# Sample tokens' C times old state: C stationary in four column strips, the turned states moving

## The reference, cut to what matters

```python
# b = sequence, l = token, g = group (8), r = head of the group (4), p = 64, n = state (128)
y_off = jnp.einsum('bclgn,bcgrpn->bclgrp', cc.astype(jnp.float32), h_prev) * jnp.exp(a_cs)[..., None]
y = (y_diag + y_off).reshape((bsz, nc * cl) + x.shape[2:])[:, :seqlen]
# and the state that goes out
h * d_c[..., None, None] + s_c
```

## Time and profile before

| | |
|---|---|
| median of 3 runs | 2480.31 us (2479.99 to 2480.95) |
| profiled execution, span | 2479.5 us |
| PE busy in it | 2237.7 us, 90% |
| DVE, ACT, POOL busy | 52%, 40%, 17% |
| mean granted clock of PE | 0.92 |
| the SSD loops | 568 to 853 us, 1783 to 2068 us |

### The profile page before, as it was taken

How to read it: one execution, slowest core, us unless ns; L and a number is a source line. 1 busy time by engine, 2 the same in 40 slices (tenths; PEclk the granted TensorE clock), 3 DMA queues, 4 the chain that set the end, 5 groups by cost and what they waited for, 6 DMA issues and landing times.

```text
span 2479.5 us, 38482 instructions
## 1 busy us (share of the span) xinstructions
PE 2237.7 (90%) x15036; PEld 2079.1 (84%) x15036; DVE 1291.6 (52%) x1936; ACT 985.0 (40%) x1121; POOL 417.0 (17%) x162
## 2 busy tenths in 40 slices
PE   7999899988898888899989989999798889869996
PEld 5999889976677788799889989898677778869996
DVE  3553546665656472454355453576665663544543
ACT  3552434253333432454255434343432334325532
POOL 2000002211222355200000000121122223640000
PEclk9999989789888889999999999897988889989998
DMA  7444543413433333344444437442233332434441
GB/s 200 160 165 139 177 149 123 132 52 103 123 92 105 96 103 126 124 158 152 155 129 159 160 120 206 137 132 84 84 99 98 105 115 71 150 107 141 162 157 65
DMA packets 258231, 317.05 MB, mean 128 GB/s; under 512 B 9070, under 2 KB 232846, under 8 KB 258010
## 3 DMA queue, kind: packets, MB, share of 16 engines
q1 hardware_dynamic: 249656, 287.92, 36.4%
q0 software_dynamic: 7776, 26.73, 3.6%
q10 hardware_dynamic: 680, 0.80, 0.1%
HBM read 291.44 MB, written 26.33 MB: 128 GB/s over the span
## 4 chain that ended last, share of the span: by engine, by line
PE 72%; DVE 11%; PEld 5%; ACT 4%; issue 3%; POOL 3%; DVEq 1%; DMA 1%; SPq 0%; PEldq 0%; ACTq 0%; POOLq 0%
PE ps L1415 18%; PE ps L1417 17%; PE ps L1416 17%; PE ps L1516 4%; POOL w_lo L1336 3%; PE ps L1836 2%; PE ps L1832 2%; ACT w_hi L672 2%; DVE a_tri L1207 2%; DVE w_lo L923 1%; PE ps L1779 1%; PEld ps L1415 1%; PEld ps L1691 1%; PE ps L1500 1%; PEld ps L1417 1%
## 5 line engine op out<-in xcount | busy, mean ns | idle before, releaser
L1415 PE MATMUL ps<-u_hi,w_hi 128*128 128x288 f32 x2736 | 866.5, 317 | 50.0 <-DVE u_lo L950 39.7
L1416 PE MATMUL ps<-u_lo,w_hi 128*128 128x288 f32 x2736 | 848.3, 310 | 0.0
L1417 PE MATMUL ps<-u_hi,w_lo 128*128 128x288 f32 x2736 | 845.1, 309 | 0.0
L672 ACT ACTIVATE w_hi<-w_raw 128x2048 fp32r<-128x2048 f32 x249 | 476.2, 1912 | 660.7 <-PE ps L1417 634.8
L923 DVE TENSOR_TENSOR w_lo<-w_raw,w_hi 128x2048 fp32r<-128x2048 f32 x172 | 394.3, 2292 | 547.2 <-ACT w_hi L672 547.1
L1415 PEld LDWEIGHTS ps<-u_hi,w_hi 128*128 128x128 f32 x2736 | 554.7, 203 | 57.3 <-issue 53.7
L1416 PEld LDWEIGHTS ps<-u_lo,w_hi 128*128 128x128 f32 x2736 | 555.8, 203 | 0.5
L1417 PEld LDWEIGHTS ps<-u_hi,w_lo 128*128 128x128 f32 x2736 | 554.8, 203 | 0.0
L1336 POOL TENSOR_TENSOR w_lo<-w_raw,w_hi 128x2048 fp32r<-128x2048 f32 x77 | 358.0, 4649 | 626.0 <-ACT w_hi L672 625.8
L1415 PE MATMUL ps<-h_hi,w_hi 128*128 (+1 forms) x704 | 209.2, 297 | 14.6 <-DVE w_lo L923 14.6
L1417 PE MATMUL ps<-h_hi,w_lo 128*128 (+1 forms) x704 | 207.9, 295 | 0.0
(11 more groups left out here) (270 smaller groups left out, 2803.6 us busy)
## 6 DMA issues: line engine op xcount, KB each, us to landing
w_raw<-in_ffn_w_dram SPq DMA_DIRECT2D x128, 1024.0 KB, 5.0
w_raw<-in_w_in_dram SPq DMA_DIRECT2D x82, 1024.0 KB, 5.3
h<-in_state_ssm_dram SPq DMA_DIRECT2D x32, 512.0 KB, 4.1
out_dram<-h POOLq DMA_DIRECT2D x32, 512.0 KB, 3.8
w_raw<-in_w_ssd_out_dram SPq DMA_DIRECT2D x16, 1024.0 KB, 4.9
kv_in<-in_cache_kv_w_dram SPq DMA_DIRECT2D x32, 256.0 KB, 4.1
w_raw<-in_w_o_dram SPq DMA_DIRECT2D x8, 1024.0 KB, 5.0
w_raw<-in_ffn_w_dram SPq DMA_DIRECT2D x8, 512.0 KB, 3.5
```

The costliest lines, as they stand in the source:

```text
L672: act.activation(w_hi[s][:], raw[s][:], ACT.Copy).then_inc(hi_ready[s].sem, 1)
L1415: pe.matmul(out, wh, hi, start=first, stop=False)
L1416: pe.matmul(out, wh, lo, start=False, stop=False)
L1417: return pe.matmul(out, wl, hi, start=False, stop=last)
```

## The change

C of all 32 sample tokens (128x32) becomes stationary, and the turned state of each of 8 sequences moves (128 columns). The output of sequence b goes to the PSUM partitions 32 x (b % 4) and up, columns 128 x (b // 4) and up, so the eight products use four column strips of PE. The 4 rows of the sequence's own tokens are wanted of each. ACT copies the 128x256 block to SBUF (tok_rows, which is h_mid's buffer), PE turns it back in two transposes, and DVE reads the own tokens' columns. L1832's products get a semaphore of their own (state_product), for which DVE's update waits instead of h0_product. PE's order changes: the turns of t=1 come before the turning back of t=0; that of t=1 is put in the middle of side(3g+2).

```diff
+    tok_rows = h_mid
@@ ScalarE
-                    for t in (2 * g, 2 * g + 1):
-                        wait(act, h0_turned, l, t + 1)
+                    for t in range(2):
+                        tile = 2 * g + t
+                        wait(act, h0_turned, l, tile + 1)
                         act.activation(h0_t[:], ps[:, 4:6, :].rearrange("p k (b c) -> p (k b) c", c=P), ACT.Copy)\
                             .then_inc(h0_t_ready.sem, 1)
-                    side(3 * g + 1)
+                        if t:
+                            side(3 * g + 1)
+                        wait(act, rows_product, l, tile + 1)
+                        act.activation(tok_rows[:], ps[:, 3 - 2 * t, 0:2 * P], ACT.Copy).then_inc(rows_ready.sem, 1)
                     side(3 * g + 2)
@@ VectorE
-                        wait(dve, h0_product, l, tile + 1)
+                        wait(dve, state_product, l, tile + 1)
                         for b in range(NB):
                             dve.scalar_tensor_tensor(out=h0[tile % 3][:, b, :], in0=h0[tile % 3][:, b, :],
...
                         dve.drain().then_inc(h_new_ready.sem, 1)
-                        dve.tensor_tensor(off_s[:, t, :], ps[:, 3 - 2 * t, 320:320 + TS], e_s[:, t, 0:TS],
-                                          ALU.mult)
+                        wait(dve, h0_product, l, tile + 1)
+                        own = ps[:, 3 - 2 * t, 0:T].rearrange("p (s j c) -> p s j c", s=2, j=4)[:, :, :, 0:NT]
+                        dve.tensor_tensor(off_s[:, t, :].rearrange("p (s j c) -> p s j c", s=2, j=4), own,
+                                          e_s[:, t, 0:TS].rearrange("p (s j c) -> p s j c", s=2, j=4), ALU.mult)
@@ TensorE
-                def side(q):
+                def side(q, between=None):
...
                     for k in range(KD):
+                        if between and k == KD // 2:
+                            between()
...
+                    def state_turn(t):
                         tile = 2 * g + t
                         wait(pe, h0_in[tile % 3], l, 16 * (tile // 3 + 1))
-                        if t:
-                            wait(pe, h0_t_ready, l, tile)
                         for b in range(NB):
                             last = turn(ps[:, 4 + b // 4, (b % 4) * P:(b % 4 + 1) * P], h0[tile % 3][:, b, :])
                         last.then_inc(h0_turned.sem, 1)
-                        if t:
-                            side(3 * g + 1)
+                    def state_products(t):
...
                         for n in range(2):
-                            pe.matmul(ps[:, 6 + n, :], xdte_s[:, t * P:(t + 1) * P],
-                                      b_diag[:, 4 * n:4 * n + 4, :].rearrange("p b n -> p (b n)"), start=True, stop=True)
+                            last = pe.matmul(ps[:, 6 + n, :], xdte_s[:, t * P:(t + 1) * P],
+                                             b_diag[:, 4 * n:4 * n + 4, :].rearrange("p b n -> p (b n)"), start=True,
+                                             stop=True)
+                        last.then_inc(state_product.sem, 1)
                         wait(pe, h0_t_ready, l, tile + 1)
                         for b in range(NB):
-                            last = pe.matmul(ps[:, 3 - 2 * t, 320 + b * NT:320 + (b + 1) * NT], h0_t[:, b, :],
-                                             fc[:, TP + b * NT:TP + (b + 1) * NT], start=True, stop=True)
-                        last.then_inc(h0_product.sem, 1)
-                    side(3 * g + 2)
+                            j, at = b % 4, b // 4 * P
+                            last = pe.matmul(ps[32 * j:32 * j + TS, 3 - 2 * t, at:at + P], fc[:, TP:T], h0_t[:, b, :],
+                                             start=True, stop=True)
+                        last.then_inc(rows_product.sem, 1)
+
+                    def rows_turn(t):
+                        wait(pe, rows_ready, l, 2 * g + t + 1)
+                        for n in range(2):
+                            last = turn(ps[:, 3 - 2 * t, n * P:(n + 1) * P], tok_rows[:, n * P:(n + 1) * P])
+                        last.then_inc(h0_product.sem, 1)
+
+                    state_turn(0)
+                    state_products(0)
+                    state_turn(1)
+                    rows_turn(0)
+                    side(3 * g + 1)
+                    state_products(1)
+                    side(3 * g + 2, lambda: rows_turn(1))
```

More of the change, by code:

```diff
@@ L452, in trunk @@
         h0_t_ready = sem("h0_t_ready", KI)
+        state_product = sem("state_product", KI)
+        rows_product = sem("rows_product", KI)
+        rows_ready = sem("rows_ready", KI)
         h0_product = sem("h0_product", KI)
@@ L1816, in _ @@
                     wait(pe, b_diag_ready, l, g + 1)
-                    for t in range(2):
+                    def state_turn(t):
                         tile = 2 * g + t
                         wait(pe, h0_in[tile % 3], l, 16 * (tile // 3 + 1))
-                        if t:
-                            wait(pe, h0_t_ready, l, tile)
                         for b in range(NB):
```

## The result

The changed kernel takes **2413.47 us** (median of 4 runs, 2411.02 to 2415.57) against 2480.15 (2478.40 to 2480.95, 4 runs) before: a ratio of 0.9729 with a 95% interval of 0.9716 to 0.9743, 66.7 us less. 2430 was forecast, in a range of 2412 to 2456. The profiled execution spans 2408.9 us.

What follows compares the result with a forecast made beforehand. PE was taken to bound the kernel except in even tails, where it waits for DVE. Per layer 3.8 + 4.4 + 9.8 + 7.5 = 25.5 us, 51 for two, gave 2429, stated as 2430 us, range 2412 to 2456.

Steps and rivals of the forecast that it cites:

- New products, turning back: On PE, each tile: L1836's 1.81 us replaced by 0.60 for products and 0.25 for turning back, saving 0.96 us.
- The ACT copy: Product rows out of PSUM, 0.37 us each: costed at nothing for t=0; 0.8 us wait in even groups' t=1, off the path.
- (d): Rival: column strips don't run beside each other, the product block takes 1.75 us; 2458 us in all; chance 0.06.
- (e): Rival: switching strips stops PE, 3.4 us a block, so the kernel gets slower, 2515 us; chance 0.04.
- The clock: Low-clock stretches behind L1836 vanish: in odd groups 1.5 us between the tiles' first L1832s and 1.5 us in side(3g+2).
- rival (a): The clock stays as it is, so 7 x 1.5 us a layer are not had: 2447 us; chance 0.17.
- Tails: From t=1's first L1832 to the next L1779: even groups gain 1.1 us (to 13.6), odd 2.1 (to 8.1, DVE late).
- Heads: L1779 to L1799: w_lo hits xdte in half a head more a layer, 2.65 us a hit, costing 1.3 us a layer.
- rival (b): w_lo hits xdte in all heads, 2 instead of half a head more a layer, 8 us: 2438 us; chance 0.15.

Runs made afterwards that it cites:

- move128: Kernel before the change, with each of L1836's matmuls moving 128 columns in place of 4 (sample y wrong): 2469.62 us, ratio 0.9955.
- one_strip_look: Changed kernel with all eight products of a tile in one column strip (sample y wrong), run again for an undisturbed profile: 2432.64 us.
- before_dve_lo: Kernel before the change, with the group-end w_lo made by DVE in the next group instead of POOL, seven of eight groups: 2400.79 us, ratio 0.9675.
- two_strips: Changed kernel with the eight products using two of the four column strips in turn (sample y wrong): 2428.08 us, one run.
- after: The changed kernel itself, against the kernel before: 2413.47 us, ratio 0.9729.
- copy_early: Changed kernel with ACT's copy of the product rows of t=1 put ahead of w_hi: 2421.46 us, ratio 0.9772 to the kernel before.
- dve_lo: Changed kernel with the group-end w_lo made by DVE in the next group, seven of eight groups: 2335.64 us, ratio 0.9416 to the kernel before.
- move128_dve_lo: Kernel before, with L1836 moving 128 columns (sample y wrong) and the group-end w_lo on DVE in seven of eight groups: 2379.97 us, ratio 0.9586.
- early_update: Kernel before the change, with only DVE's state update waiting for L1832's products instead of L1836's: 2468.59 us, ratio 0.9947.

## Why the prediction was right, and by how much not

The forecast of 2430 gave a gain 15.7 us too small, and the 2413.5 measured lie 1.5 us above the low end of its range. 8.9 of the 15.7 are in the loops, 6.8 outside them. By mechanism the terms held, but two errors about the heads cancelled, as shown below, and that was luck.

**New products, turning back: right.** 0.60 us for the block was right as time on PE (0.58), though not by its own working: the matmuls are 0.025 us apart, which makes 0.41 us for 16, and 0.17 us go by before the first turn behind them. With 0.2 us for turning back, X0 to X1 falls by 7.92 - 6.92 = 1.00 us where no clock is in play; 0.96 was forecast. The ACT copy at t=0 is hidden, at t=1 of even groups PE waits 0.34 us for it (0.8 was forecast), off the path. Rivals (d) and (e) are out: strips work at once, and a change to strips and back costs at most that 0.17 us.

On this the Trainium skill, "TensorEngine Tiling (Array Packing)", Key Properties, says that a change of tiling mode drains TensorE. The row ahead of the block shows nothing of it: L1843 to L1850 is 612.67 - 610.76 = 1.91 us, as L1832 to L1836 was the earlier trace rows, though the shape of the weights changes there too (32 rows to 128), so this shows only that the strips add nothing. If it is the 0.17 us behind the block, it is an eighth of what rival (e) needed to turn the sign (a block of 1.93 us in place of 0.60).

**The clock: right in mechanism, and a little more than counted.** Both low stretches of odd groups went, so rival (a) is out, and move128 shows the cause. X0 to X1 of odd groups gave 18.8 against 19.6. Even groups gave 11.1 against 7.6, since one of them had stood at 11.08 us before; I had read one even group and taken it for all. The 4.1 and 4.4 us in odd heads and between L1799 and X0 had been costed at nothing, though both are the clock behind a wait. In odd heads the wait ahead stood at L1779 (4.39 us) and stands at the turns now (3.68 us at 595.04), so a part of the half clock is spent in the turns, and L1791 takes 3.15 us where L1779 took 3.49. The 4.4 us belong to the even heads, next.

**Tails: right.** Even 13.6 against 13.6, with L1292 held and the wait at the turns, as described; odd 8.04 against 8.1, with DVE late at L1791 by 0.27 us where 0.3 was forecast.

**Heads: the mechanism right, the count too small and the price too high.** w_lo was to hit xdte in half a head more a layer. It hit in four of six heads (12.7 to 13.4 us) where it had been one of six: three more in both layers instead of one, and -6.3 us instead of -2.6. That is two thirds of the way to rival (b). But 2.65 us a hit, the difference of two heads, left out what follows a head. Where w_lo holds b_diag instead, PE waits late, at L1811, and the half clock behind that wait stretches L1811 to X0:

```profile
636.31 1.10 PE L1811 MATMUL ps<-dec,xdt 128*64 128x128 f32 x16 [2.93 <-DVE dec_s L1258]
...
641.74 1.98 PE L1843 MATMUL ps<-b_diag,xdte_s 32*128 32x512 f32 x4
```

That is 5.43 us, and 5.3 to 5.4 in every head of this kind before and after, against 3.78 where w_lo hit xdte. From L1779 to X0 a hit costs 17.26 - 16.15 = 1.1 us before and 0.9 after. (In one_strip_look four of six heads of this kind were followed by 3.8 us, so the stretch isn't always slow.) The 4.4 us gained between L1799 and X0 come with the three more hits: together the even heads lost 1.9 us where 2.6 were forecast. Three times the hits at well under half the price gave nearly the forecast sum. Where DVE is late by 0.3 us the two outcomes lie side by side, and no row that I had from the trace before could say which.

**What no step had.** 59.9 of 66.7 us are in the loops. The median less the loops is 1917.9 us before and 1911.0 after. In the other kernels, whose code outside the loops is the same, it is 1908.6 (before_dve_lo) to 1920.1 (two_strips), with no order by what was changed. In the profiles the stretch ahead of the first loop lasts 566.3 to 574.1 us, and from 300 us on its clock is 0.82 to 0.97 in different places. What sets this for a kernel was not tried and stays open. A median of this kernel therefore can't credit an edit in the loop with less than some 10 us. The loops in the profile see less of it, but they are read in one execution of each kernel, and the two loops of one execution, the same code, differ by 2.7 us in after, 2.9 in before_dve_lo and 5.6 in copy_early, but by 0.5 us or less in dve_lo and move128_dve_lo, where the clock is 1.00 throughout. The split into 29.2 and 38.6 us is good to about 3 us, an estimate from these differences.

## What to carry to other kernels

In this kernel, products with few moving columns behind full weight loads cost twice: the loads are paid (0.113 us each), and the half-rate clock that follows most of the blocks is paid in whatever comes next. Turning the product round, so that the wide operand moves and the narrow ones sit beside each other in column strips, took both away. Before crediting an edit with the time that it frees, look where the next engine stands: here an elementwise operation on POOL, tied to DVE, cost more time (78 us) than the change gave (67 us).

## What the runs showed of the hardware

- Column strips are independent down to the matmul: starts are 0.11 us apart in one strip, 0.053 in two, 0.025 in four, with 128 x 32 fp32 weights loaded for each.
- The granted clock fell to its lower level (1.2 GHz) behind 22 of the 32 blocks of 16 full weight loads with 4 moving columns each, though PE's record shows no gap, and behind none of 32 with 128 moving columns (move128). Why the other ten were spared stays open.
- w_lo takes 4.5 us on POOL and 2.27 us on DVE. While POOL runs it, DVE's L1292 (0.25 us alone) lasts until w_lo ends, 4.65 to 5.38 us in after and 3.94 where it started 0.66 us behind w_lo (one_strip_look), and a_tri takes 6.8 in place of 1.7.
- A DVE operation that the record shows 0.62 us ahead of POOL's w_lo was still held (593.33 and 593.95), and so were those 0.76 (742.22 and 742.98) and 0.81 us ahead (782.12 and 782.93 in after); one 0.94 us ahead was not (664.66 and 665.60 in early_update). The Trainium skill, "SBUF — State Buffer", Who interferes with whom, says that a DVE instruction with two SBUF inputs contends with a GpSimd instruction that reads SBUF, and that the order of issue decides who blocks. That L1292, which has two, is held until w_lo ends, the rows show; which was issued first can't be read from the recorded starts here.
